# A value added during the PSUM evacuation, half sums moved from GpSimd to VectorE, and later split steps, in a fused stick-breaking attention layer on one Trainium2 core

## What is computed

```python
def stick_breaking_attention(q, k, v):
    scale = 1.0 / math.sqrt(Dh)
    for t0 in range(0, S, BLOCK):
        kend = t0 + BLOCK
        z = einsum('bthd,bshd->bhts', q[:, t0:kend], k[:, :kend]) * scale
        mask = s_idx < t_idx
        log_beta = log_sigmoid(z)
        log_rem = where(mask, log_sigmoid(-z), 0.0)
        after = cumsum(log_rem, axis=3, reverse=True) - log_rem
        w = where(mask, exp(log_beta + after), 0.0)
        outs.append(einsum('bhts,bshd->bthd', w, v[:, :kend]))

h = rmsnorm(x, a_norm)
q, k, v, g = split(h @ w_in, 4)
o = stick_breaking_attention(q, k, v)
x = x + (o * silu(g)) @ w_out
return rmsnorm(x, final_norm)
```

## Time and profile before

| | |
|---|---|
| median of 3 runs | 1680.17 us (1679.1 to 1680.67) |
| the profiled execution's own time | 1680.25 us |
| its span in the trace | 1678.5 us |
| granted TensorE clock over the span | 0.998 of full speed |
| TensorE matmul busy | 98% of the span, 8600 matmuls |
| VectorE busy | 80% |
| ScalarE busy | 54% |
| GpSimd busy | 14% |

### The profile page before, as it was taken

The page is one execution under the profiler, slowest core; times in us unless marked ns, Lnnn a source line. Parts: engine busy times, 40 slices in busy tenths (PEclk is TensorE's granted clock), DMA queues, the critical chain, the costliest instruction groups (busy, mean ns, idle before and its releaser), DMA issues.

```text
span 1678.5 us, 23276 instructions
## 1 busy us (share of the span) xinstructions
PE 1649.8 (98%) x8600; PEld 1377.5 (82%) x8600; DVE 1338.3 (80%) x1879; ACT 906.1 (54%) x1773; POOL 235.0 (14%) x212
## 2 busy tenths in 40 slices
PE   7999999999999999999999999999999999999998
PEld 6888878888888888888888888888888888778786
DVE  4436478889898889888988988898888888956765
ACT  6625355565565555656555655665555556661222
POOL 0020012110211011102110211011101110008400
PEclk9999999999999999999999999999999999999999
DMA  9858634342524243334333342425243434398732
GB/s 293 273 159 266 199 119 138 101 148 67 152 75 132 78 143 98 104 101 120 111 97 109 105 133 68 138 82 145 64 136 95 127 92 146 120 357 282 238 138 100
DMA packets 162785, 237.09 MB, mean 141 GB/s; under 512 B 49776, under 2 KB 90736, under 8 KB 162672
## 3 DMA queue, kind: packets, MB, share of 16 engines
q1 hardware_dynamic: 93184, 160.02, 30.4%
q10 hardware_dynamic: 69488, 75.58, 15.1%
HBM read 155.78 MB, written 79.76 MB: 140 GB/s over the span
## 4 chain that ended last, share of the span: by engine, by line
PE 85%; DVE 4%; DMA 4%; ACT 2%; POOL 2%; issue 1%; SPq 1%; ACTq 0%; DVEq 0%
PE proj_ps L714 28%; PE turn_ps L741 13%; PE proj_ps L674 11%; PE z_ps L731 7%; PE z_ps L732 7%; PE o_ps L755 7%; PE o_ps L756 7%; PE turn_ps L785 3%; PE z_ps L785 2%; POOL w_raw L650 1%; DMA gate<-gate_cols 1%; PE proj_ps L785 1%; DMA wo_raw<-in_w_out 1%; DVE u L1125 1%; DMA w_raw<-in_w_qkg 1%
## 5 line engine op out<-in xcount | busy, mean ns | idle before, releaser
L903 ACT ACTIVATE u<-z_ps 128x512 f32<-128x512 f32 (+3 forms) x640 | 341.8, 534 | 409.1 <-PE z_ps L732 405.2
L1125 DVE TENSOR_TENSOR_SCAN u<-u,u 128x512 f32<-128x512 f32 x384 | 491.8, 1281 | 0.0
L1130 DVE TENSOR_TENSOR r_turned_lo<-turn_ps,r_turned_hi 128x512 fp32r<-128x512 f32 (+3 forms) x640 | 377.5, 590 | 34.7 <-ACT r_turned_hi L909 33.0
L909 ACT ACTIVATE r_turned_hi<-turn_ps 128x512 fp32r<-128x512 f32 (+3 forms) x640 | 340.2, 532 | 60.2 <-issue 43.0
L650 POOL TENSOR_SCALAR w_raw<-w_raw,a_norm_col 128x128 f32<-128x128 f32 x192 | 176.7, 938 | 1207.4 <-DMA w_raw<-in_w_qkg 1207.4
L741 PE MATMUL turn_ps<-ident,u 128*128 128x128 f32 x2176 | 342.9, 273 | 0.0
L714 PE MATMUL proj_ps<-hT_hi,w_hi 128*128 128x512 f32 x768 | 320.2, 417 | 0.0
L714 PE MATMUL proj_ps<-hT_lo,w_hi 128*128 128x512 f32 x768 | 320.0, 417 | 0.0
L714 PE MATMUL proj_ps<-hT_hi,w_lo 128*128 128x512 f32 x768 | 319.8, 416 | 0.0
L741 PEld LDWEIGHTS turn_ps<-ident,u 128*128 128x128 f32 x2176 | 267.8, 140 | 58.9 <-DVE u L1125 0.2
L755 PE MATMUL o_ps<-r_turned_hi,dv_head 128*128 128x512 f32 (+3 forms) x640 | 231.5, 362 | 8.0 <-DVE r_turned_lo L1130 3.8
(11 more groups left out here) (106 smaller groups left out, 1645.6 us busy)
## 6 DMA issues: line engine op xcount, KB each, us to landing
x_T<-in_xT SPq DMA_DIRECT2D x32, 512.0 KB, 5.9
qk_hi_cols<-made_hi ACTq DMA_DIRECT2D x64, 256.0 KB, 2.8
qk_lo_cols<-made_lo ACTq DMA_DIRECT2D x64, 256.0 KB, 3.2
w_raw<-in_w_qkg SPq DMA_DIRECT2D x24, 512.0 KB, 3.4
x_rows<-in_x SPq DMA_DIRECT2D x16, 512.0 KB, 4.5
v_rows<-v_stage ACTq DMA_DIRECT2D x32, 256.0 KB
v_here<-v_rows SPq DMA_DIRECT2D x64, 128.0 KB, 2.9
v_next<-v_rows SPq DMA_DIRECT2D x64, 128.0 KB, 3.1
```

Of the source, the lines that this page charges most:

```text
L903: nc.scalar.activation(u_t[(m // CB) % RU][STEPS[m][3]][:, 0:w], z_ps[m % RZ][:, 0:w], ACT.Sigmoid, scale=-Z_SCALE).then_inc(s_u, 1)
L909: nc.scalar.activation(rt_hi[m % RT][:, 0:w], t_ps[m % RT][:, 0:w], ACT.Copy).then_inc(s_hi, 1)
L1125: nc.vector.tensor_tensor_scan(u, u, other, start, ALU.mult, op).then_inc(s_r, 1)
L1130: nc.vector.tensor_tensor(rt_lo[m % RT][:, 0:w], t_ps[m % RT][:, 0:w], as_f32(rt_hi[m % RT][:, 0:w]), ALU.subtract).then_inc(s_lo, 1)
```

## The change

- **First values.** `vT` becomes 64 rows (the features of a head) for each of 16 heads instead of 128 rows for 8 tiles, with zeros in rows 64 to 127 (a memset on VectorE at the start). TensorE turns the first value rows by 16 transposes in place of 8. `empty` adds the values: the copy of 128 x 512 becomes four ACTIVATEs of 128 x 128 (Identity), each with a column of `vT` as bias. `piece_start` and GpSimd's addition are gone.
- **Half sums.** The sum of the two output parts of groups 2 to 7 goes from GpSimd to VectorE (`group_sum`). GpSimd has no work left in the output stage. VectorE's loop now takes `group_sum` and `gated` of group t+1, then the first residual and norm block, then `gated_low`, then the second block.
- **Pieces.** Pieces 0 to 2 are placed at steps 609, 612 and 615 in place of 605, 609 and 613. The gate follows the sum in the same step; high comes one step later, low two steps later.
- **Weights.** `out_weight_high` of slice k runs six steps after its load, at steps 629 to 636.

```diff
 WO_AT = {WO_FROM + k: k for k in range(KT)}
+WO_HIGH_AT = {WO_FROM + 6 + k: k for k in range(KT)}
@@
-PIECE_STEP = [SHORT_FROM + 4, SHORT_FROM + 8, SHORT_FROM + 12, LAST_K_FROM + 4] + [REST_FROM + at for at in (6, 7, 8, 10)]
-LAST_PIECE_STEP = PIECE_STEP[-1] + 4
+PIECE_STEP = [SHORT_FROM + 8, SHORT_FROM + 11, SHORT_FROM + 14, LAST_K_FROM + 4] + [REST_FROM + at for at in (6, 7, 8, 10)]
+LAST_PIECE_STEP = PIECE_STEP[-1] + 2
 SUM_AT = {n: i for i, n in enumerate(PIECE_STEP)}
-GATE_AT = {n + 2: i for i, n in enumerate(PIECE_STEP)}
-LOW_AT = {n + 4: i for i, n in enumerate(PIECE_STEP)}
+HIGH_AT = {n + 1: i for i, n in enumerate(PIECE_STEP)}
+LOW_AT = {n + 2: i for i, n in enumerate(PIECE_STEP)}
@@
-                for t in range(2, TG):
-                    pool.wait_ge(s_in[t % RG], 48 * (t // RG + 1))
-                    nc.gpsimd.tensor_tensor(oa[t % RG][:], oa[t % RG][:], ob[t % RG][:], ALU.add).then_inc(s_sum, 1)
-                    pool.wait_ge(s_sum, t - 1)
-                    blocks = oa[t % RG][:].rearrange("p k (b t) -> p k b t", t=P)
-                    start_v = vT[:, :, t * GB:(t + 1) * GB].unsqueeze(3).to_broadcast([P, KT, GB, P])
-                    nc.gpsimd.tensor_tensor(blocks, blocks, start_v, ALU.add).then_inc(s_start, 1)
@@
-                for k in range(KT):
-                    last = nc.tensor.transpose(t_ps[2][:, k * NB:(k + 1) * NB], v_first[:, k * P:(k + 1) * P], ident[0:NB, 0:NB])
+                for h in range(H):
+                    last = nc.tensor.transpose(t_ps[2][0:DH, h * NB:(h + 1) * NB], v_first[:, h * DH:(h + 1) * DH], ident[0:NB, 0:NB])
@@ def empty(e):
-                    nc.scalar.activation(o_st[e % RO][:], o_ps[:], ACT.Copy).then_inc(s_ost, 1)
+                    for r in range(CB):
+                        b = c * CB + r
+                        last = nc.scalar.activation(o_st[e % RO][:, r * P:(r + 1) * P], o_ps[:, r * P:(r + 1) * P], ACT.Identity,
+                                                    bias=vT[:, h, b:b + 1])
+                    last.then_inc(s_ost, 1)
@@ scalar
-                nc.scalar.activation(vT[:].rearrange("p k b -> p (k b)"), t_ps[2][:, 0:KT * NB], ACT.Copy).then_inc(s_vT, 1)
+                nc.scalar.activation(vT[0:DH].rearrange("p h b -> p (h b)"), t_ps[2][0:DH, 0:H * NB], ACT.Copy).then_inc(s_vT, 1)
+                act.wait_ge(s_vT, 1)
+                act.wait_ge(s_below, 1)
@@
-                    if n in SUM_AT:
-                        piece_start(SUM_AT[n])
-                    if n in GATE_AT:
-                        piece_high(GATE_AT[n])
-                    if n - 4 in WO_AT:
-                        out_weight_high(WO_AT[n - 4])
+                    if n in HIGH_AT:
+                        piece_high(HIGH_AT[n])
+                    if n in WO_HIGH_AT:
+                        out_weight_high(WO_HIGH_AT[n])
@@ vector
+                def group_sum(t):
+                    dve.wait_ge(s_in[t % RG], 48 * (t // RG + 1))
+                    nc.vector.tensor_tensor(oa[t % RG][:], oa[t % RG][:], ob[t % RG][:], ALU.add).then_inc(s_sum, 1)
@@
                     if t + 1 < TG:
+                        group_sum(t + 1)
                         gated(t + 1)
-                        gated_low(t + 1)
                     for n in range(GB * (t - 1), GB * t):
                         if n:
                             residual(n, 0)
                             residual(n, 1)
                         norm_block(n)
+                        if n % GB == 0 and t + 1 < TG:
+                            gated_low(t + 1)
```

More of the change, by code:

```diff
@@ L47 @@
 AT_VT = BASE + 90 * KB
-AT_SMALL = AT_VT + 512
+AT_SMALL = AT_VT + KB
 AT_WV = [(BASE, BASE + 16 * KB), (BASE + 32 * KB, BASE + 48 * KB)]
@@ L294, in all_stages @@
         unbroken = place(nc, "unbroken", [P, CH], F32, AT_MASK)
-        vT = place(nc, "v_first_T", [P, KT, NB], F32, AT_VT)
+        vT = place(nc, "v_first_T", [P, H, NB], F32, AT_VT)
         wo_hi = place(nc, "wo_hi", [P, KT, D], F32R, AT_WO_HI)
@@ L353, in all_stages @@
         s_vT = sem("v_first_ready")
+        s_below = sem("v_first_zeros_below_ready")
         s_wraw = sems("w_raw_loaded", 2)
@@ L386, in all_stages @@
         s_psum = sem("piece_summed")
-        s_pstart = sem("piece_started")
         s_pgated = sem("piece_gated")
@@ L390, in all_stages @@
         s_plow = sem("piece_lo_ready")
-        s_sum = sem("group_parts_added")
-        s_start = sem("group_started")
+        s_sum = sem("group_summed")
         s_gated = sem("group_gated")
@@ L911, in empty @@
                 def empty(e):
+                    h, c = e // NC, e % NC
                     act.wait_ge(s_o, e + 1)
@@ L922, in store_o @@
                     act.dma_start(o_lo[rows, cols], o_st[e % RO][DH:P, :]).then_inc(s_oout[e % RO], 16)
[L926 to L935, removed]
                 def piece_high(i):
@@ L1143, in piece_gate @@
                     t, k = i // PIECES, piece_ks(i)
-                    dve.wait_ge(s_pstart, i + 1)
+                    dve.wait_ge(s_psum, i + 1)
                     nc.vector.tensor_tensor(oa[t][:, k, :], oa[t][:, k, :], gt[t][:, k, :], ALU.mult).then_inc(s_pgated, 1)
@@ L1150, in piece_low @@
                     nc.vector.tensor_tensor(m_lo[t][:, k, :], oa[t][:, k, :], as_f32(m_hi[t][:, k, :]), ALU.subtract).then_inc(s_plow, 1)
+                def group_sum(t):
+                    dve.wait_ge(s_in[t % RG], 48 * (t // RG + 1))
+                    nc.vector.tensor_tensor(oa[t % RG][:], oa[t % RG][:], ob[t % RG][:], ALU.add).then_inc(s_sum, 1)
                 def gated(t):
-                    dve.wait_ge(s_start, t - 1)
+                    dve.wait_ge(s_sum, t - 1)
                     nc.vector.tensor_tensor(oa[t % RG][:], oa[t % RG][:], gt[t % RG][:], ALU.mult).then_inc(s_gated, 1)
@@ L1181, in _ @@
                 nc.vector.memset(zeros[:], 0.0).then_inc(s_zero, 1)
+                nc.vector.memset(vT[DH:P], 0.0).then_inc(s_below, 1)
                 wv_low(0, 0)
@@ L1233, in _ @@
                         piece_sum(SUM_AT[n])
-                    if n in GATE_AT:
-                        piece_gate(GATE_AT[n])
+                        piece_gate(SUM_AT[n])
                     if n in LOW_AT:
```

## The result

| | before | changed |
|---|---|---|
| median | 1678.73 us (6 runs) | 1687.48 us (6 runs, 1684.91 to 1690.18) |
| profiled execution, its span | 1680.25, 1678.5 us | 1687.96, 1686.2 us |

The ratio is 1.0050, 95% interval 1.0039 to 1.0060: slower by 0.5%, or 8.4 us. The forecast was slower, by 3.8 us, less than half of what came.

A forecast was written before the change was run, and what follows sets the result against it. TensorE's matmul stream, filling 98% of the span, was taken as the bound. The terms 8.7 + 1.3 + 0.6 - 2.8 - 4.2 + 0.2 gave +3.8 us on 1680.25, so 1684.0 us, range 1677.0 to 1692.0.

The forecast's parts named there:

- Part 1: Four ACTIVATEs at 62 chunk ends take 1.17 us, 0.57 more than the copy, delaying TensorE's next weighted sum: +8.7 us.
- nothing: DMA issues and next L909 behind the chunk-end copy come later, but feed work two steps (some 4 us) later: no cost.
- The additions' price: At each chunk end: 365 ns per ACTIVATE from PSUM with a bias column, 1.17 us for four; the skill's 1.27 rejected.
- Part 2: Last two chunk ends and weights: the first output matmul waits for the late weight slice, 1492.5 against 1491.24, +1.3 us.
- the half clock: Upper bound at the last chunk's weights: +3.2 in place of +1.3 if the two waits also halve TensorE's clock.
- The last end: Very end of the attention: TensorE resumes 0.09 us after the last copy, nothing in hand, so +0.6 us.
- Part 3: Pieces moved four steps later: 3.3 us of waits can go, 0.5 given back for VectorE, -2.8 us.
- the last of the rivals: The pieces' stall moves with them, VectorE short at steps 609 to 617: up to +2.8 us; no separate chance.
- Part 4: Output stage: group 3's 2.28 us wait and the 1.9 us half-clock stretch go, low part about 30 us ahead: -4.2 us.
- Part 5: Kernel start: sixteen transposes for eight, a 256-column copy and a wait for it, +0.2 us (0 to 0.7).
- L934's price: Rival at the chunk ends: the four additions cost 1.28 us as L934's do, giving 1689 us; chance 0.20.
- The free column: Rival at the chunk ends: the bias column costs nothing, group only 0.22 us longer, sum -5.0, 1675 us; chance 0.13.

The follow-up runs named there:

- e3: Kernel before, its copy at each chunk end cut into four ACTIVATEs adding a column of zeros; 1690.57 us, ratio 1.0060 to before.
- e2: Kernel before, its copy at each chunk end cut into four copies of 128x128 without a bias column; 1681.90 us, ratio 1.0010 to before.
- e1: Changed kernel with one 128x512 copy at each chunk end in place of the four additions, first values left out; 1676.03 us, ratio 0.9976 to before.
- e4: Changed kernel with the sums of groups 2 to 7 on GpSimd again; 1687.45 us, ratio 1.0041 to before.
- e12: Changed kernel with the low part of group t+1 ahead of the norm blocks again; 1686.21 us, ratio 1.0038 to before.
- e9: Kernel before with only the new order: low part behind the first norm block in the output stage; 1682.71 us, ratio 1.0013 to before.
- e8: Kernel before with late pieces, waits per weight slice, sums on VectorE, low part later, first values on ScalarE in the output stage; 1672.60 us, ratio 0.9958.
- e7: Changed kernel, output projection waiting for each slice of the weights' high part separately, not all eight at once; 1682.90 us, ratio 1.0021 to before.
- e10: e8 with the low part of group 2 ahead of the first norm block; 1675.89 us, ratio 0.9969 to before.
- e6: Changed kernel with pieces 0 to 2 back at steps 605, 609 and 613; 1689.73 us, ratio 1.0049 to before.
- e5: Changed kernel with the weight slices split at steps 627 to 634 again; 1685.57 us, ratio 1.0032 to before.
- e11: e10 with a semaphore for each slice of the weights' low part as well; 1675.08 us, ratio 0.9971 to before.

## Why the prediction was right, and where it was off

The direction and the mechanism of the loss (late chunk ends, past what TensorE has in hand) held. The size did not: the sum was 3.8 us against 7.7 in the traces and 8.4 by the ratio. No term of the sum had the wrong sign; the terms for the gains were a little too large and two of those for the losses too small. Step by step:

- **Part 1, chunk ends, +8.7.** The group lasts 1.14 us (forecast 1.17), and a late copy costs what the shortfall to 0.15 us says: the gap of 0.47 lost 0.24. By that rule and the measured 1.14 us, the gaps of before give 7.2 us in all. Over the 62 ends the distances of starts at L747 and L748 grew by 7.5 us, in 40 of them by more than 0.03.
- **The same stretch, beyond the chunk ends.** It grew by 9.7 us, of which its own 59 ends are 7.0; 2.7 are waits elsewhere. The forecast put them at nothing ("what they feed is used two steps (some 4 us) later: nothing"). The column alone brings part of it: beyond the ends e3 lost 1.1 us against before, where e2 gained 0.4, one trace each. Another part is not from the additions. Two waits, 0.62 us for `u` at 927 and 1.04 for a low part at 935, stand behind a DMA issue on ScalarE's queue that took 1.79 us. The same issue took 1.85 us in e1, which has no additions, and 1.09 to 1.77 in the five others made from the change; it took 0.56 or 0.57 in before and the six made from it, e3 with its column among them. So the long issue is not the four instructions' doing, and in e1 the same two places lost 0.7 us without them; what such an issue meets stands in the last section, and no row of before could tell of it. Over all traces the six kernels with a bias column besides the change took 1160.4 to 1164.0 us for this stretch (the change 1162.0), the six without one 1151.1 to 1152.8, and e1 1154.3.
- **The additions' price:** 371 ns per instruction where the Trainium skill ("ScalarE: Activation LUTs", section on what ACT_TABLE_LOAD costs) gives 387, and 1.14 us for four where it gives 1.27: the measurement decides, and the rows of before were nearer. Its 93 ns for each pointer operand agrees: 372 less 285 is 87.
- **Part 2, last chunk, +1.3.** This is the term that was mis-sized most: +3.3. The walk gave the waits to within 0.4 us, but the half clock that I had only as the upper bound (+1.9) did come (1.6). The last end is +0.5 (forecast 0.6).
- **Part 3, pieces, -2.8:** -2.5 in their chunk, and +0.7 in the next two, where VectorE is late at steps 616 and 617. The 0.5 that was given back for VectorE was too little: together -1.8. This is the last of the rivals, in small.
- **Part 4, output stage, -4.2:** -4.0, both the wait and the clock. Its reason was partly wrong. Neither the new order nor the sum's move was needed by itself, only one GpSimd pass fewer (e4, e12, e9). What ended the wait at group 3 was not the low part but the residual behind it on VectorE, as the earlier trace rows name it (L1165, ending 0.6 us after the low part). And the low part of group 3 lies 17 us ahead in the change, not 30.
- **Part 5, +0.2:** +0.1.

That the total came out at twice the forecast and still in the range is the width of the range, which the rivals had set. That it came as high as it did is in part chance: 0.7 to 1.7 us of it stand behind the one DMA issue. The step that the forecast had wrong in kind is the "nothing" for what comes behind the copy; the step that was wrong in size is Part 2, 1.3 us for what cost 3.3.

Of the rivals, L934's price (1689 us) lay nearest in time, for the wrong reason: its 1.28 us per group did not occur. The free column is ruled out by e2 and e3.

## What to carry to other kernels

Where one engine's stream is the bound, an instruction on another engine is free only up to the time its consumer has in hand at that point: here a copy of 0.60 us could grow by 0.2, not by 0.55, sixty-four times, on an engine that was idle 46% of the time. Work moved out of a busy inner loop into a stage where its engine is mostly idle costs little: four instructions with a column at each chunk end cost 10.1 us (e3), while e8, with the same additions in the output stage, is 7.1 us faster than before, though one group still waits 1.97 us there. (Its other gains are in that number too, such as the waits per slice, worth 4.9 us in e7.) Where the moved work stands in the order still counts, as e10 shows. Read waits of a pipelined engine by the distance of starts, since short ones do not show as idle time.

## What the runs showed of the hardware

- Between the first 100 us and the last matmul, eleven of the 14 traces have a stretch of 3.4 us at half clock (0.50 to 0.52; 6.8 us in e4). It cost 1.5 to 1.7 us (2.7 in e4). It began between 0.7 us before and 1.5 us after the end of a wait. Such waits lasted, by starts, 2.01 us (e6, in the middle of the attention, at 1348.8), 2.28 (before), 2.29 (e1), 2.46 (e10), 2.47 (e5), 2.60 to 2.69 (the change, e3, e4, e6 again, e12), 3.09 (e11) and 4.2 (e9). No such stretch followed waits of 1.97 (e8), 1.99 and 2.20 us (before), about 2.1 (e3, e11), 2.25 (e9), nor one of 2.50 (e2). So between 2.0 and 2.5 us both occur: the length of the wait does not decide it alone, and what does stays open. Such a wait can cost nearly twice its length.
- A DMA issue on ScalarE's queue mostly takes 0.33 to 0.64 us, but two to five in each trace, after the first 200 us, took 1.0 to 2.2 us, 49 in the 14 traces. 46 of these 49 overlap in time with a transfer of the queue that the page of each profile lists as "q8 instruction" (16 KB each), which moves data in under 5% of that time. But 11 to 17 ordinary issues in each trace overlap with one as well, so that this is the cause is likely and not shown. The long issue at 924 stands in all seven kernels made from the change and in none of those made from the kernel before. While such an issue lasted, ScalarE began nothing else: in the change, the next ACTIVATE after 924.05 began at 926.42.
